# A scan's wait for W moved from its first to its second step, and a third of a threshold search's counts moved from ScalarE to VectorE

## What is computed

```python
# the recurrence, per head, over blocks of the sequence
v_new = u_i - w_i @ state
o     = qg @ state + a_i @ v_new
state = state * gl + kd.T @ v_new

# the selection, per block of queries
score = where(causal, sum_j relu(q_j . k) * w_j, -inf)
_, idx = lax.top_k(score, 256)
```

## Time and profile before

| | us |
|---|---|
| median of 3 runs | 865.08 (862.08 to 866.42) |
| the profiled execution | 863.28 |
| its span, first instruction to last | 861.5 |
| PE, busy | 764.0 (89%) |
| DVE, busy | 494.5 (57%) |
| ACT, busy | 462.0 (54%) |
| POOL, busy | 145.3 (17%) |
| mean granted clock of PE | 0.955 of full speed |

### The profile page before, as it was taken

How to read it: one execution, slowest core, us unless ns; L and a number is a source line. 1 busy time by engine, 2 the same in 40 slices (tenths; PEclk the granted TensorE clock), 3 DMA queues, 4 the chain that set the end, 5 groups by cost and what they waited for, 6 DMA issues and landing times.

```text
span 861.5 us, 11407 instructions
## 1 busy us (share of the span) xinstructions
PE 764.0 (89%) x3996; PEld 620.6 (72%) x3996; DVE 494.5 (57%) x1068; ACT 462.0 (54%) x1045; POOL 145.3 (17%) x248
## 2 busy tenths in 40 slices
PE   6999969899987999699996999895698998998975
PEld 5888857778876888578895788773476676774764
DVE  5634869756664475544655378763556556536532
ACT  4523566888768875788677852224443334323300
POOL 0000000053021510242101520001002033212330
PEclk9999989999998999899997999997989999999988
DMA  9312110124001320014000241008401122111201
GB/s 357 100 49 75 49 37 26 37 65 141 25 26 49 96 86 25 21 60 127 25 25 25 88 131 49 25 25 266 148 1 49 37 86 86 49 50 61 74 25 49
DMA packets 56424, 60.87 MB, mean 71 GB/s; under 512 B 16048, under 2 KB 42928, under 8 KB 55984
## 3 DMA queue, kind: packets, MB, share of 16 engines
q1 hardware_dynamic: 56368, 60.15, 21.3%
HBM read 45.46 MB, written 14.68 MB: 70 GB/s over the span
## 4 chain that ended last, share of the span: by engine, by line
PE 62%; DVE 19%; ACT 11%; issue 6%; DMA 1%; SPq 0%; POOL 0%; DVEq 0%; ACTq 0%; POOLq 0%
PE bank L846 15%; PE bank L854 9%; PE bank L856 9%; PE bank L855 9%; PE bank L860 3%; ACT cst L1658 3%; PE bank L1090 2%; PE bank L1118 2%; PE bank L1010 2%; DVE score L1280 2%; PE bank L1025 2%; PE bank L997 2%; PE bank L1023 2%; DVE mix_lo L1525 1%; DVE arena L1489 1%
## 5 line engine op out<-in xcount | busy, mean ns | idle before, releaser
L854 PE MATMUL bank<-x_hi,ring_split 128*128 128x512 f32 x480 | 200.9, 419 | 7.4 <-DVE x_lo L1225 7.3
L855 PE MATMUL bank<-x_lo,ring_split 128*128 128x512 f32 x480 | 191.6, 399 | 0.0
L856 PE MATMUL bank<-x_hi,ring_split 128*128 128x512 f32 x480 | 191.6, 399 | 0.0
L1658 ACT ACTIVATE cst<-score,sel 128x1024 bf16<-128x1024 f32 (+2 forms) x192 | 166.9, 873 | 29.0 <-DVE sel L1302 27.6
L854 PEld LDWEIGHTS bank<-x_hi,ring_split 128*128 128x128 f32 x480 | 93.2, 194 | 23.4 <-DVE ring_split L1233 7.2
L856 PEld LDWEIGHTS bank<-x_hi,ring_split 128*128 128x128 f32 x480 | 92.8, 193 | 20.8
L855 PEld LDWEIGHTS bank<-x_lo,ring_split 128*128 128x128 f32 x480 | 93.2, 194 | 15.6
L1759 ACT ACTIVATE arena<-arena,misc 128x512 f32<-128x512 f32 (+7 forms) x32 | 24.8, 775 | 81.0 <-DVE misc L1495 81.0
L1575 ACT ACTIVATE arena<-bank 128x512 f32<-128x512 f32 (+1 forms) x108 | 49.8, 499 | 34.3 <-PE bank L860 9.7
L846 PE MATMUL bank<-w_out_hi,mix_hi 128*128 128x512 f32 x128 | 56.0, 438 | 6.7 <-DVE mix_lo L1525 4.2
L1545 DVE SCALAR_TENSOR_TENSOR arena<-qkvT,bank 128x512 f32<-128x512 f32 x16 | 11.0, 688 | 80.0 <-PE bank L846 80.0
(11 more groups left out here) (247 smaller groups left out, 1438.9 us busy)
## 6 DMA issues: line engine op xcount, KB each, us to landing
ring<-in_w_groups SPq DMA_DIRECT2D x30, 512.0 KB, 3.5
x_raw<-in_x_t SPq DMA_DIRECT2D x8, 512.0 KB, 9.3
side_z<-stage SPq DMA_DIRECT2D x16, 256.0 KB, 2.1
w_out_sb<-in_wout_t SPq DMA_DIRECT2D x2, 2048.0 KB, 13.0
zgT<-side_z SPq DMA_DIRECT2D x8, 512.0 KB, 3.9
qkvT<-in_x SPq DMA_DIRECT2D x8, 512.0 KB, 4.7
out_y<-arena SPq DMA_DIRECT2D x8, 512.0 KB, 2.8
ring<-in_wmem_t SPq DMA_DIRECT2D x2, 1024.0 KB, 4.7
```

What stands on the lines that cost most here:

```text
L854: nc.tensor.matmul(dst, hi, xh, start=(c == 0), stop=False)
L855: nc.tensor.matmul(dst, hi, xl, start=False, stop=False)
L856: last = nc.tensor.matmul(dst, lo, xh, start=False, stop=(c == KT - 1))
L1658: sc.activation(signs[order[e] % 2][:, 0:w], score[:, score_at(b):score_at(b + 1)], ACT.Sign, scale=-1.0, bias=candidate[:, b - 2:b - 1], ...
```

## The change

Two edits. The wait for W (the release of the bank of `nw`) is taken from the first matmul of V at blocks 0 and 4. It stands now ahead of the second matmul, at blocks 1 and 4; block 0 has no second matmul. And the counts of the group (5, 4), of 768 and 640 keys, are made by DVE: one `tensor_scalar` that compares with the candidate (is_lt), writes the flags as bf16 into a stretch of the constants that nothing reads, and adds them up. Each of them is linked: the next DVE instruction that needs one waits for its end. They stand at the place in the plan where the ACT counts stood. `update` waits for four ACT counts an iteration. The constant of blocks 4 and 5 is changed to fit a count of ones, where the others sum signs.

```diff
--- before.py
+++ after.py
@@ -51,6 +51,8 @@
 FLOAT_BITS = 32
 
 COUNT_GROUPS = ((7, 2), (6, 3), (5, 4))
+DVE_COUNTED = COUNT_GROUPS[-1]
+N_ACT_COUNTS = 4
 NLEV = 7
 BASE = 16
 LEV0 = 4
@@ -123,7 +125,7 @@
     plan = []
     add = plan.append
 
-    selection = [[("count", it, b) for b in group] for it in range(FLOAT_BITS) for group in COUNT_GROUPS]
+    selection = [[("dve_count" if group == DVE_COUNTED else "count", it, b) for b in group] for it in range(FLOAT_BITS) for group in COUNT_GROUPS]
     selection += [[("reach", 7), ("reach", 2)], [("reach", 6), ("reach", 3)], [("reach", 5), ("reach", 4), ("threshold",)]]
     selection += [[("dm", b, i), ("dm", b, i + 1)] for b in (3, 4, 2, 5, 6, 7) for i in (0, 2, 4)]
 
@@ -139,7 +141,7 @@
             group = selection.pop(0)
             for e in group:
                 add(e)
-            if group[-1][0] == "count" and group[-1][2] == COUNT_GROUPS[-1][-1]:
+            if group[-1][0] == "dve_count" and group[-1][2] == COUNT_GROUPS[-1][-1]:
                 due.append(("update", group[-1][1]))
             done += 1
         return done
@@ -550,6 +552,7 @@
             sel[:, i * N_SEL:(i + 1) * N_SEL] for i in range(10))
 
         signs = [cst[:, C_KT + i * 512:C_KT + (i + 1) * 512].bitcast(BF16) for i in range(2)]
+        dve_flags = cst[:, C_LEV:C_LEV + 384].bitcast(BF16)
         eps_rms, eps_ln, one1 = misc[:, 16:17], misc[:, 17:18], misc[:, 18:19]
         mxp, nmx = misc[:, 20:28], misc[:, 28:32]
         sums, rinv = misc[:, 32:40], misc[:, 40:48]
@@ -787,7 +790,7 @@
                         sp.dma_start(row(a, R_Y).rearrange("p (b c) -> p b c", b=4), half_of(diag_y, a)).then_inc(y_base_loaded, 16)
                 if e == ("reach", 7):
 
-                    sp.wait_ge(keys_counted, N_SEL * FLOAT_BITS)
+                    sp.wait_ge(keys_counted, N_ACT_COUNTS * FLOAT_BITS)
                     sp.dma_start(cst[:, C_KT:C_BIT], consts[:, C_KT:C_BIT]).then_inc(kt_sem, 16)
 
             sp.wait_ge(*filled(last_use[groups[-1]]))
@@ -1038,13 +1041,13 @@
                     h, b = e[1:]
                     a, i = b // 4, b % 4
                     key = ("V", h, b)
-                    if i == 0:
-                        pe.wait_ge(*released(("nw", h, a)))
                     if not first(key):
                         pe.wait_ge(*vacated(key))
                     last = nc.tensor.matmul(ps(key)[:, 0:P], blk(row(a, R_Y), i), blk(row(a, R_VB), i), start=True, stop=(b == 0))
                     if b:
 
+                        if b == 1 or i == 0:
+                            pe.wait_ge(*released(("nw", h, a)))
                         pe.wait_ge(*released(("S", h, b - 1)))
                         last = nc.tensor.matmul(ps(key)[:, 0:P], blk(row(a, R_NW), i), dn_s[:, (b % 2) * P:(b % 2 + 1) * P], start=False, stop=True)
                     last.then_inc(fill_of(key), 1)
@@ -1215,7 +1218,7 @@
             v.memset(candidate, 0.0)
             for b in range(2, NB):
 
-                v.memset(n_half[:, b - 2:b - 1], (b + 1) * P - 2 * TOPK + 0.5)
+                v.memset(n_half[:, b - 2:b - 1], (b + 1) * P - (1 if b in DVE_COUNTED else 2) * TOPK + 0.5)
             v.memset(eps_ln, LN_EPS).then_inc(small_constants_set, 1)
             for e in plan:
                 k = e[0]
@@ -1280,9 +1283,16 @@
                         last = v.scalar_tensor_tensor(score[:, at + lo:at + hi], r[:, 0:hi - lo], w,
                                                       score[:, at + lo:at + hi], ALU.mult, ALU.add)
                     last.then_inc(scores_summed, 1)
+                elif k == "dve_count":
+                    it, b = e[1:]
+                    w = (b + 1) * P
+                    if it == 0:
+                        dve.wait_ge(scores_summed, order["idx", b, IXH - 1, len(idx_chunks(b)) - 1])
+                    link(v.tensor_scalar(dve_flags[:, 0:w], score[:, score_at(b):score_at(b + 1)], candidate[:, b - 2:b - 1], 0.0, ALU.is_lt, ALU.add,
+                                         accum_out=n_low[:, b - 2:b - 1]))
                 elif k == "update":
                     it = e[1]
-                    dve.wait_ge(keys_counted, N_SEL * (it + 1))
+                    dve.wait_ge(keys_counted, N_ACT_COUNTS * (it + 1))
                     link(v.tensor_tensor(n_off, n_low, n_half, ALU.subtract))
                     if it == 0:
```

## The result

The changed kernel takes **880.8 us** (median of 4 runs, 878.45 to 883.36) where the kernel before takes 864.28 (median of 4) on the same chip: a ratio of 1.0201, with a 95% interval of 1.0181 to 1.0222. It is slower by 2.0% (1.8 to 2.2), 16.5 us between the medians; 877 was forecast, with a range from 866 to 887. The profiled execution of the changed kernel is the slowest of its four, 883.36 us with a span of 881.6, so a comparison of the two traces has to explain 20.1 us of span, 3.6 more than the medians differ by. Where these 3.6 come from is not shown.

The account below looks back on a forecast made before the run. PE, busy 89% of the span, was taken as the bound. Heads +8.7, clock +7.05, small waits -4.1 and end +1.0 made +12.7 us: 876.0 from the profiled 863.28, 877.8 from the median; forecast 877, range 866 to 887.

Parts of the forecast that it names:

- A pair takes 1.96 us: DVE's counts of 768 and 640 keys in one iteration: 1.96 us with read-outs and links, bounds 1.35 and 2.4.
- The rival with the plain rate: DVE's counts run at the plain comparison's rate, 1.35 us a pair: +8 us in all, 872; chance 0.07.
- The heads: +2.9 each: At each of three heads' gaps: +3.9 for pairs, +0.2 ahead of the gap, -1.2 for W; three times +8.7 us.
- the pairs' 3.9: At each gap, one pair ahead of the candidate's `update` and one ahead of the state's first copy: +3.92 us.
- the W edit's 1.2: At each of three gaps, ACT no longer waits 1.23 us for PE's projection: gain 1.2 us a head.
- the W edit does nothing: At the gaps, O's bank waits for the same copy: +1.2 us a head, 880; 0.10 of the forecast's chance.
- The clock: 7.05: After the new second wait in each head, PE's granted clock of 0.50 falls on the path: 2.0, 2.0 and 3.05 us.
- the clock stays up: PE's burst in the gap splits the idleness, so no slow clock: +5.7 us, 870; chance 0.10.
- The small waits in the scans: -3.3: In the scans, pairs fit DVE's idleness, `update` and state come sooner, five PE waits for V's bank shrink: -3.3 us.
- The start of the search: -0.8: At 176.33, ACT's copies of transposed keys come sooner, removing PE's wait of 0.80 us: -0.8.
- worse: DVE falls behind in the levels too, PE waiting 2 us more at three places a head: +18, 895; chance 0.10.
- The end: +1.0: At the search's end, DVE reaches its long selection later, PE waiting for the level's result: 0 to +2.0, taken +1.0.

## Why the prediction was right, and where it was not

**The verdict and its cause.** Slower, by DVE's place in front of PE: shown. The pairs at the gaps cost 9.8 us taken out and 10.7 put in, of 16.5.

**A pair takes 1.96 us.** It takes 1.97 (369.27 to 371.24 above), and the means of the 32 say the same. The rival with the plain rate is out. The trace also bears out what was said of the Trainium skill there: its tier table (VectorE: DVE Perf Modes, "The perf-mode tier table") gives `tensor_scalar` on fp32 in SBUF two elements a cycle, and that does not carry over to a comparison that accumulates, at 1005 ns for 768 elements with bf16 output as with f32.

**The heads: +2.9 each.** The same matmul of the second step, ahead of which both kernels have done the same work, is 7.7, 15.1 and 18.4 us late in heads 0, 1 and 2. Less the lateness just ahead of each gap (4.7, 12.1 and 15.4, the table's columns 250, 345 and 440) that is 3.0 in each. Here the terms held: the pairs' 3.9 (3.9 to 4.0 by the run without them), and the W edit's 1.2 (1.25 in its own trace). The waits stand where they were expected, 4.16 us ahead of S (about 4 forecast) and 6.05 ahead of the second step (8 forecast; the wait of 1.16 for O's bank between them takes part of it). The rival "the W edit does nothing" named 880, nearer to the measured 880.8 than 877 is, but its reason is not there: with the counts alone these 3.0 us are 4.2.

**The clock: 7.05.** The mechanism was right, with 0.50 granted behind each of the three waits. The lateness grew by 2.5, 2.3 and 1.7 us in those stretches, 6.4 in all. The loss comes with the W edit: it moves the slow stretch onto the path, and the counts alone lose 1.6 us there over three heads. The rival "the clock stays up" is out.

**The small waits in the scans: -3.3.** Half right. In the second and third head the waits for the bank of V are gone, and between the slow stretch and the next levels the changed kernel gets back 2.0 and 1.9 us. In head 0 it loses 1.9 instead: PE waits 1.16 us at 290.58 for the bank of V and 1.13 at 306.86 for V's copy, each behind a pair on DVE (iterations 10 and 12). Together -2.0. What the prediction called the cover, DVE's idleness while it waited for a count, was read at one place of the second head and taken for every scan step.

**The start of the search: -0.8. Here the prediction went wrong.** The wait for ACT of 0.80 us at 176.33 went, as forecast. But I looked there only for what ACT's relief would bring and had no term for what DVE does between 185 and 215, since PE showed no wait for DVE there. In the kernel before, DVE's copy to the stage begins at

```profile
188.62 0.69 DVE L1261 COPY stage<-bank 128x512 f32<-128x512 f32 x1
```

and ends about 1.1 us before PE takes the bank for a projection (190.45). In the changed kernel a pair stands ahead of it, and the `update` behind the pair:

```profile
187.47 1.00 DVE L1291 TENSOR_SCALAR_CACHE_REDUCE cst<-score,sel 128x768 bf16<-128x768 f32 x1
...
190.81 0.69 DVE L1264 COPY stage<-bank 128x512 f32<-128x512 f32 x1
```

The copy comes 2.2 us later, and PE's projection waits 1.75 us for its bank. Measured: +4.0 us by the run without these pairs and +4.05 by the run with these alone. The rival "worse" had this mechanism, with 2 us at three places of each head, and argued against it that PE showed no wait for DVE before. That argument is wrong: a wait of nothing says nothing about how much slack there is.

**The end: +1.0.** The lateness grows by 2.0 us after 500, at the term's upper bound, but not by the term's mechanism. PE's wait for the level's result after the search is what it was (1.21 us, at 540.49), and between 510 and 560 the lateness does not grow at all. The growth comes later, and the W edit alone has 0.9 us of it too. Its cause is open; that the term was of the right size is luck.

**The sum.** By the parts of the trace: 0.2 ahead of the search, 4.5 at its start, 8.9 in the heads, 6.4 for the clock, -2.0 in the scans, 2.0 at the end, 20.1 in all; forecast were nothing, -0.8, 8.7, 7.05, -3.3 and 1.0. So the two large terms held, and the start was 5.3 us too low. With the start alone put right (+4.0 by the run without its pairs, for -0.8), 12.7 + 4.8 = 17.5 against 16.5 between the medians. That the forecast of 877 lay within 4 us rests on the heads and the clock.

## What to carry to other kernels

Before work is moved to an engine with room to spare, ask for each place what stands behind it in that engine's queue and whether the busiest engine waits for that: the same 2 us pair cost 1.8 us ahead of V's and the state's copy (10.7 / 6), 0.7 at the start (4.05 / 6), and brought 0.6 on the mean in the later scan steps (5.7 / 9). That an engine is not waited for now is no measure of its slack; look at the idle time ahead of the instruction that must not be late. And when PE waits at the end of a queue, try the order of the queue before its length: a few entries of the plan moved in each of three heads took off 17.5 us (867.2 to 849.7), while moving all 32 pairs off ACT cost 13.6 (867.2 to 880.8). An order has to be tried, not only argued: the next step in the same direction cost 8 us.

## What the runs showed of the hardware

The split of a ring buffer, a subtraction with both inputs in SBUF on DVE, takes 1.22 us. Near 198 us of the changed kernel it took 3.76, while POOL worked through a copy and two multiplications of its own:

```profile
198.31 3.76 DVE L1236 TENSOR_TENSOR ring_split<-ring,ring_split 128x1024 fp32r<-128x1024 f32 x1 [1.87 <-ACT ring_split L1585]
```

```profile
197.85 0.62 POOL L1878 COPY arena<-arena 64x256 f32<-64x256 f32 x1
198.44 2.54 POOL L1830 TENSOR_TENSOR arena<-arena,cst 128x512 f32<-128x512 f32 x2
```

It ended at 202.07, 1.1 us after POOL. In the kernel with the first six pairs alone POOL ended at 200.72 and the split at 201.80; in the W edit alone at 199.13 and 200.21. In each it ends nearly one split's length after POOL, whenever it began: DVE does not slow down, it stands still until POOL is done. It also goes the other way. Where the split begins first, it keeps its 1.22 us, and POOL's small subtraction beside it, 0.31 to 0.32 us for this shape at 192.69 and 297.32, takes 1.37. DVE's row comes first, then POOL's:

```profile
402.95 1.22 DVE L1236 TENSOR_TENSOR ring_split<-ring,ring_split 128x1024 fp32r<-128x1024 f32 x1 [1.44 <-ACT ring_split L1585]
```

```profile
402.98 1.37 POOL L1877 TENSOR_TENSOR arena<-arena 64x64 f32<-64x64 f32 x1
```

The Trainium skill (SBUF — State Buffer, "SBUF: two separate sides") calls it an exclusive lock for DVE instructions with two SBUF inputs beside POOL, held by whoever starts first; the trace agrees in both directions: near 198 us POOL's copy is already running when the split begins, at 402.95 the split begins first. (The two starts there are 0.03 us apart, and POOL's spans are rough.) The convolutions, which read two inputs from SBUF too, show it in small: L1388 takes 1.41 us at 365.71, beside POOL, and 0.75 at 377.87. The new counts, with one source, keep their 1.00 and 0.88 us everywhere, also the 25 of the 64 that run beside a POOL instruction. The pairs ahead moved DVE's and POOL's work further onto each other near 198 us; how much of the 4 us at the start comes from this and how much from the queue was not tried apart.
